# The forget gate's block between the two query blocks of a two-layer kernel, and a new order of VectorE's and ScalarE's work after it

## The chip, the cores and the metric

One core of one Trainium2 chip runs the whole kernel. The metric is the time on the device in microseconds (us); lower is better.

## The reference, cut to what matters

Two transformer blocks run one after the other on 512 tokens of width 1024, in float32. The change lies at the start of the second block, where its input `x` (the first block's normed output) is normed again and multiplied by the large matrix `w_in`:

```python
h = rms_norm_2(x, norm_mix_g[l])
proj = h @ w_in[l]
cb, cc, cin, q, k, v, f_logit, g_logit = jnp.split(proj, split_idx, axis=-1)   # widths 512 x6, 8, 2048
u = causal_dwconv(cc * cin, conv_mix_w[l])
y_conv = (cb * u) @ w_out_conv[l]
log_f = jax.nn.log_sigmoid((f_logit + b_f[l]).astype(jnp.float32))
o = forgetting_attention(q, k, v, log_f)        # adds F[query] - F[key], F = cumsum(log_f)
gates = jax.nn.sigmoid(g_logit + b_gate[l])
```

## The kernel before, in words

**Tiling.** Tokens lie along the free dimension (`xT`, 8 chunks of 128 features by 512 tokens). The weights pass in *slabs*, numbered in the order in which TensorE uses them. A whole A slab holds 1024 rows by 256 columns, a half one 512 rows by 256 columns. Every float32 product is made of three matmuls on rounded parts: a slab comes by DMA, ScalarE rounds it into `w_hi` (L975), VectorE subtracts to get `w_lo` (L1521), and TensorE multiplies hi x hi, hi x lo and lo x hi. `w_hi` and `w_lo` hold four half slabs each, as a ring: `MIX_FREES[e]` names the slabs whose place in the ring slab `e` gives back, so they are split only once slab `e` is finished (`slab_done`), and TensorE waits for `w_lo_ready` ahead of each slab.

**Order around the change.** Each engine's program is written out by hand, in one strict order, and the engines meet by semaphores. On TensorE: two key slabs (S_K2, S_K2+1), two sums of squares, query slab S_Q2, `turn_row` (four matmuls of one column, into bank 7), query slab S_Q2+1, the forget gate's slab S_F2 (1024 rows by 128 columns, 24 matmuls of 512 columns; bank 6), and then the *pairs*. A pair `i` is 512 output columns computed in seven half slabs p0 to p6 of 24 matmuls of 256 columns each (a Strassen-like scheme that saves one product in eight), with the order p0,i p3,i-1 p2,i p5,i-1 p1,i p6,i-1 p4,i. Pairs 0 to 2 are `cc`, `cin` and `cb`, 3 to 6 the gates. Within pair 5 four whole slabs `out,0` to `out,3` (24 matmuls of 512 columns each) multiply by `w_out_conv`. The values' slab S_V2 and the attention follow.

**What a pair needs.** The products p1, p3, p4, p5 work on sums of blocks of the gained input `xg2` (four subtractions at L1968 to L1974, rounded by ScalarE at L1235 into `s2_hi`, the rest by VectorE at L1978 into `s2_lo`). The weights of p1, p3 and p6 of a pair are made by accumulating DMAs on GpSimd's queue (L905): each adds to the slab before it in the chain p0, p1, p3, p6, and waits for that slab's `w_lo`; p5 adds to p4 in the same way. VectorE recombines: after p2 it writes one part from PSUM (L2013, `z_n0`), which p0 of the next pair waits for; after p3, `z_rest` (L2018) and `z_m0` (L2020), which p1 of the next pair waits for; after p5, `z_rest2` (L2024) and `z_m1` (L2027), for which ScalarE's copy of the next pair's p1 out of PSUM (L1218, `z_k1`) waits, and p4 waits for that copy; after p6, `z_n1` (L2032).

**What else VectorE does there.** It makes 1/rms of the new norm (L1943, L1945, the reciprocal L1544 `inverse(N_MIX2)`), scales keys (L1958) and queries (L1960) out of PSUM, forms the forget gate's log-sigmoid and its running sum (L1981 to L1992, with ScalarE's Abs, Exp and Ln at L1238 to L1242, after a table load), makes the final norm's reciprocal (`inverse(N_FINAL)`, L1544) and applies it to `xT` (`x_normal`, L1951), multiplies `cc` by `cin` (L2071), and adds the taps of the convolution (`taps`, L2048 and L2050), each at a place of the pairs' loop given by `X_NORMAL_AT` and `TAPS_AT`.

Of the kernel before, what the change touches and what calls it, by code (L numbers as in the profile page):

```python
# [20 lines left out]
P = 128  # L21
# [132 lines left out]
S_Q2 = _cols_a("w_in_2", 3 * WIDTH, WIDTH)  # L154
S_F2 = _add("w_in_2", "A", 0, DC, F_AT, P)
# [49 lines left out]
X_NORMAL_AT = {("p2", 0): (0, 1), ("p4", 0): (2, 3), ("p0", 1): (4, 5), ("p2", 1): (6, 7)}  # L205
TAPS_AT = {("p4", 2): 0, ("p0", 3): 1, ("p2", 3): 2}
# [61 lines left out]
def _z_landed(kind, i, stage):  # L268
# [23 lines left out]
for _s in range(N_SLABS):  # L292
    _inner = (_s in (S_V + 1, S_V2 + 1)
              or S_FFN + 1 < _s < S_DOWN
              or S_MIX <= _s < S_V2
# [71 lines left out]
def two_blocks(nc, t, out):  # L367
    with ExitStack() as ctx:
# [316 lines left out]
        def _(sp):  # L685
# [273 lines left out]
        def _(act):  # L959
# [240 lines left out]
            split_w(S_K2 + 3)  # L1200
# [41 lines left out]
            A(fsum[:, 1], fsum[:, 1], ACT.Ln, bias=1.0).then_inc(f_ln, 1)  # L1242
            for e in range(S_MIX, S_V2):
# [5 lines left out]
                if (kind, i) == ("p4", FIRST_GATE):  # L1249
# [238 lines left out]
        def _(dve):  # L1488
# [464 lines left out]
            for s in range(S_K2, S_F2):  # L1953
                finished(s)
                c0 = (s - S_K2) % 2 * 2
                for j in range(2):
                    if s < S_Q2:
                        ins = V.tensor_tensor(k2[:, c0 + j], bank(s, j), both, ALU.mult)  # L1958
                    else:
                        ins = V.scalar_tensor_tensor(q2[:, c0 + j], bank(s, j), SCALE, both, ALU.mult, ALU.mult)  # L1960
                free(ins)
                if s >= S_Q2:
                    for f in MIX_FREES[s]:
                        split_w(f)
                if s == S_Q2 - 1:
                    dve.wait_ge(xg_ready, 2 * DC)
                    h00, h01, h10, h11 = xg2_block(0, 0), xg2_block(0, 1), xg2_block(1, 0), xg2_block(1, 1)
                    V.tensor_tensor(h11, h01, h11, ALU.subtract).then_inc(sums_made, 1)  # L1968
                    dve.wait_ge(sums_made, 5)
                    V.tensor_tensor(h01, h01, h00, ALU.subtract).then_inc(sums_made, 1)  # L1970
                    dve.wait_ge(sums_made, 6)
                    V.tensor_tensor(h00, h00, h11, ALU.subtract).then_inc(sums_made, 1)
                    dve.wait_ge(sums_made, 7)
                    V.tensor_tensor(h10, h10, h00, ALU.subtract).then_inc(sums_made, 1)  # L1974
                if s == S_Q2:
# [1099 lines left out]
```

## Time and profile before

| | |
|---|---|
| three timed runs | 1266.15, 1271.99, 1279.71 us, median 1271.99 |
| the profiled execution | 1270.42 us, of which 1268.7 us are the span of the profile |
| TensorE busy in the span | 97% |
| mean granted clock of TensorE | 0.994 of full speed |

The profile is of one execution. Its times are counted from the span's start. TensorE's columns are *PE* (matmuls) and *PEld* (weight loads); DVE is VectorE, ACT ScalarE, POOL GpSimd, SP SyncE. A matmul's end is modelled, so the distance between the starts of two matmuls is what counts.

### The profile page before, as it was taken

The numbers are of one execution on the slowest core, as the hardware profiler recorded it, in microseconds if no ns is written. First come the engines' busy times: TensorE is split into PE (matmuls) and PEld (weight loads), VectorE is DVE, ScalarE is ACT, GpSimd is POOL, SyncE is SP. The second block draws the span as 40 slices with busy tenths as digits, with TensorE's granted clock in tenths as the row PEclk, the third lists the DMA queues.
The fourth block names the chain that finished last, engine by engine and source line by source line (L and its number), as shares of the span: only waits on it lengthen the run. The fifth ranks groups of instructions, "written<-read, shape, count | busy, mean of one in ns | idle before, by whom it ended". The sixth has DMA issues, their size and how long they took to land.

```text
span 1268.7 us, 19160 instructions
## 1 busy us (share of the span) xinstructions
PE 1235.8 (97%) x7805; PEld 1084.5 (85%) x7805; DVE 993.8 (78%) x1199; ACT 668.4 (53%) x832; POOL 185.9 (15%) x168
## 2 busy tenths in 40 slices
PE   6999999999999999999999999999999999999997
PEld 5778777889999999997899999657888999998886
DVE  6788764878878688987889867566678898979896
ACT  5462674374445346557433535363344665656555
POOL 4003010002222111200212212000000222201020
PEclk9999999999999999999899999999999999999999
DMA  5422201259999589653499957301324798958765
GB/s 170 141 67 100 67 1 34 97 138 182 198 183 187 114 239 280 107 114 117 86 197 189 194 100 193 122 3 34 116 84 149 132 211 186 178 141 180 211 111 138
DMA packets 144442, 174.14 MB, mean 137 GB/s; under 512 B 5354, under 2 KB 118234, under 8 KB 144226
## 3 DMA queue, kind: packets, MB, share of 16 engines
q0 software_dynamic: 58288, 71.33, 34.8%
q1 hardware_dynamic: 86050, 101.58, 23.9%
q8 instruction: 62, 1.02, 0.3%
q14 instruction: 26, 0.21, 0.1%
q10 hardware_dynamic: 16, 0.00, 0.0%
HBM read 170.78 MB, written 2.11 MB: 136 GB/s over the span
## 4 chain that ended last, share of the span: by engine, by line
PE 86%; DVE 7%; ACT 4%; issue 2%; DMA 1%; DVEq 0%; SPq 0%; ACTq 0%
PE psum L2456 11%; PE psum L2458 11%; PE psum L2457 11%; PE psum L2719 10%; PE psum L2721 10%; PE psum L2720 10%; PE psum L2791 3%; PE psum L2793 3%; PE psum L2792 3%; PE psum L2993 2%; PE psum L2994 2%; PE psum L2995 2%; PE psum L2902 1%; PE psum L2594 1%; PE psum L2579 1%
## 5 line engine op out<-in xcount | busy, mean ns | idle before, releaser
L975 ACT ACTIVATE w_hi<-raw 128x1024 fp32r<-128x1024 f32 (+2 forms) x121 | 157.2, 1301 | 214.8 <-PE psum L2458 148.9
L1521 DVE TENSOR_TENSOR w_lo<-raw,w_hi 128x1024 fp32r<-128x1024 f32 (+2 forms) x121 | 185.7, 1536 | 58.5 <-ACT w_hi L975 58.5
L2456 PE MATMUL psum<-act_hi,w_hi 128*128 128x512 f32 x520 | 209.1, 402 | 5.9 <-DVE act_lo L1530 1.7
L2458 PE MATMUL psum<-act_hi,w_lo 128*128 128x512 f32 x520 | 205.5, 395 | 0.0
L2457 PE MATMUL psum<-act_lo,w_hi 128*128 128x512 f32 x520 | 204.5, 393 | 0.0
L2719 PE MATMUL psum<-s_hi,w_hi 128*128 128x256 f32 x704 | 195.5, 278 | 1.3 <-issue 1.3
L2721 PE MATMUL psum<-s_hi,w_lo 128*128 128x256 f32 x704 | 195.2, 277 | 0.0
L2720 PE MATMUL psum<-s_lo,w_hi 128*128 128x256 f32 x704 | 195.1, 277 | 0.0
L2719 PE MATMUL psum<-act_hi,w_hi 128*128 128x256 f32 x528 | 147.6, 280 | 3.0 <-DVE conv_p L2013 2.7
L2720 PE MATMUL psum<-act_lo,w_hi 128*128 128x256 f32 x528 | 147.1, 279 | 0.0
L2721 PE MATMUL psum<-act_hi,w_lo 128*128 128x256 f32 x528 | 147.1, 279 | 0.0
L2719 PEld LDWEIGHTS psum<-s_hi,w_hi 128*128 128x128 f32 x704 | 132.1, 188 | 1.7 <-issue 1.4
L2721 PEld LDWEIGHTS psum<-s_hi,w_lo 128*128 128x128 f32 x704 | 132.2, 188 | 0.0
L2720 PEld LDWEIGHTS psum<-s_lo,w_hi 128*128 128x128 f32 x704 | 132.0, 187 | 0.2
L2456 PEld LDWEIGHTS psum<-act_hi,w_hi 128*128 128x128 f32 x520 | 98.4, 189 | 32.5 <-issue 6.7
L2457 PEld LDWEIGHTS psum<-act_lo,w_hi 128*128 128x128 f32 x520 | 98.4, 189 | 22.8 <-issue 1.7
L2458 PEld LDWEIGHTS psum<-act_hi,w_lo 128*128 128x128 f32 x520 | 98.3, 189 | 21.1
L2719 PEld LDWEIGHTS psum<-act_hi,w_hi 128*128 128x128 f32 x528 | 99.9, 189 | 3.9 <-issue 3.6
L2720 PEld LDWEIGHTS psum<-act_lo,w_hi 128*128 128x128 f32 x528 | 99.7, 189 | 0.3
L2721 PEld LDWEIGHTS psum<-act_hi,w_lo 128*128 128x128 f32 x528 | 99.9, 189 | 0.0
L1521 DVE TENSOR_TENSOR w_lo<-xz,w_hi 128x1024 fp32r<-128x1024 f32 x60 | 73.3, 1221 | 26.2 <-ACT w_hi L975 26.1
L975 ACT ACTIVATE w_hi<-xz 128x1024 fp32r<-128x1024 f32 x60 | 63.4, 1057 | 42.5 <-PE psum L2721 23.1
(413 smaller groups left out, 2690.3 us busy)
## 6 DMA issues: line engine op xcount, KB each, us to landing
raw<-in_w_in SPq DMA_DIRECT2D x16, 1024.0 KB, 5.2
xz<-in_w_ffn_in POOLq DMA_DIRECT2D x24, 512.0 KB, 6.4
raw<-in_w_ffn_in SPq DMA_DIRECT2D x22, 512.0 KB, 5.1
xz<-in_w_up POOLq DMA_DIRECT2D x21, 512.0 KB, 6.0
raw<-in_w_up SPq DMA_DIRECT2D x18, 512.0 KB, 5.0
raw<-in_w_in SPq DMA_DIRECT2D x15, 512.0 KB, 5.2
v<-in_w_in POOLq DMA_DIRECT2D x15, 512.0 KB, 6.5
x_buf<-in_w_ffn_out POOLq DMA_DIRECT2D x6, 1024.0 KB, 9.9
```

What stands on the lines that cost most here:

```text
L975: A(w_at(w_hi, s, h, n - h), home(s, n)[:, h:n], ACT.Copy).then_inc(w_hi_ready, 1)
L1521: V.tensor_tensor(w_at(w_lo, s, h, n - h), home(s, n)[:, h:n], w_at(w_hi, s, h, n - h).bitcast(F32), ALU.subtract).then_inc(w_lo_ready, 1)
L2456: mm(dst, stationary[0], moving[0], start=first, stop=False)
L2457: mm(dst, stationary[0], moving[1], start=False, stop=False)
L2458: return mm(dst, stationary[1], moving[0], start=False, stop=last)
L2719: mm(dst, wh, hi, start=kind not in ("p2", "p4") and k == 0 and m == 0, stop=False, skip_group_check=True)
L2720: mm(dst, wh, lo, start=False, stop=False, skip_group_check=True)
L2721: ins = mm(dst, wl, hi, start=False, stop=True, skip_group_check=True)
L2791: mm(dst, wh, hi, start=fresh, stop=False, skip_group_check=True)
L2792: mm(dst, wh, lo, start=False, stop=False, skip_group_check=True)
L2793: return mm(dst, wl, hi, start=False, stop=True, skip_group_check=True)
L2993: mm(dst, hi, wh, start=fresh, stop=False, skip_group_check=True)
```

## The change

The forget gate's slab S_F2 moves from behind the second query slab to between the two; its weights land in a place of their own (`v2[:, 2:4]`) instead of `raw`. The second query slab becomes two half slabs (S_Q2B and the next), computed by `quarter_slab`, in banks 0 and 1, as before. `turn_row` moves behind S_F2. VectorE and ScalarE follow a new order: VectorE splits S_F2 and the first half of the second query slab before the rms; then both keys, two splits, the first queries, the forget gate's start, the sums of `xg2`, and the rest of the gate between the `s2_lo` operations, which now come in the order 0, 3, 2, 1. ScalarE does its part of the forget gate ahead of rounding the sums. In the pairs, `inverse(N_FINAL)` moves from behind p1,0 to behind p4,0, `x_normal` from p2,0 p4,0 p0,1 p2,1 (two chunks each) to p0,1 (two), p4,1 and p0,2 (three each), the last taps from p2,3 to p4,3, the convolution's last product from p6,2 to p0,4, and its splitting from p4,3 to p5,3 (ScalarE) and p1,4 (VectorE). TensorE's order and its waits in the pairs are the same. At the end, S_V2's first products take their banks in the order 0, 2, 3, 1, and only bank 1 waits for `z_rest2`.

```diff
 S_K2 = _cols_a("w_in_2", 4 * WIDTH, WIDTH)
-S_Q2 = _cols_a("w_in_2", 3 * WIDTH, WIDTH)
-S_F2 = _add("w_in_2", "A", 0, DC, F_AT, P)
+S_Q2 = _cols_a("w_in_2", 3 * WIDTH, COLS_A)
+S_F2 = _add("w_in_2", "A", 0, DC, F_AT, P, ("z", ("f", 0), 2))
+S_Q2B = _add("w_in_2", "A", 0, WC, 3 * WIDTH + COLS_A, COLS_A)
+_add("w_in_2", "A", WC, WC, 3 * WIDTH + COLS_A, COLS_A)
...
-X_NORMAL_AT = {("p2", 0): (0, 1), ("p4", 0): (2, 3), ("p0", 1): (4, 5), ("p2", 1): (6, 7)}
-TAPS_AT = {("p4", 2): 0, ("p0", 3): 1, ("p2", 3): 2}
+X_NORMAL_AT = {("p0", 1): (0, 1), ("p4", 1): (2, 3, 4), ("p0", 2): (5, 6, 7)}
+TAPS_AT = {("p4", 2): 0, ("p0", 3): 1, ("p4", 3): 2}
+LO_ORDER = (0, 3, 2, 1)
...
+    if g == GROUP[S_F2]:
+        return OUT_BANKS[0]
+    if g == GROUP[S_Q2B]:
+        return bank_of(GROUP[S_K2 + 1])
     return 2 if g == GROUP[S_Q2] else 4 * (g % 2)
...
-            for s in range(S_K2, S_MIX):
+            for s in (S_K2, S_K2 + 1, S_Q2, S_Q2B):
                 load_slab(s)
             sp.wait_ge(slab_done, S_K2)
+            for s in (S_F2, S_Q2B + 1):
+                load_slab(s)
...
-                        sp.wait_ge(w_lo_ready, S_Q2 + 2 + i)
+                        sp.wait_ge(w_lo_ready, S_Q2B + 2 if i else S_Q2B + 1 if kind == "p4" else S_K2 + 2)
...
-            split_w(S_K2 + 3)
+            split_w(S_F2)
+            split_w(S_Q2B)
...
-            for s in range(S_Q2, S_MIX):
-                for f in MIX_FREES[s]:
-                    split_w(f)
-                if s == S_Q2:
-                    for k, (kh, th) in enumerate(SUM_PLACE):
-                        act.wait_ge(sums_made, 4 + k + 1)
-                        A(s2_hi[k].rearrange("p (k n) -> p k n", k=WC), xg2_block(kh, th), ACT.Copy).then_inc(sums_hi_ready, 1)
+            for f in MIX_FREES[S_Q2]:
+                split_w(f)
...
+            for k, (kh, th) in enumerate(SUM_PLACE):
+                act.wait_ge(sums_made, 4 + k + 1)
+                A(s2_hi[k].rearrange("p (k n) -> p k n", k=WC), xg2_block(kh, th), ACT.Copy).then_inc(sums_hi_ready, 1)
+            for s in range(S_F2, S_MIX):
+                for f in MIX_FREES[s]:
+                    split_w(f)
...
-                if (kind, i) == ("p4", FIRST_GATE):
+                if (kind, i) == ("p5", FIRST_GATE):
...
             for s in (S_K2, S_K2 + 1):
                 finished(s)
                 split_w(s + 2)
+            split_w(S_Q2B)
...
-            for s in range(S_K2, S_F2):
...
-                if s >= S_Q2:
-                    for f in MIX_FREES[s]:
-                        split_w(f)
-                if s == S_Q2 - 1:
...
-                if s == S_Q2:
...
+            keys(S_K2)
+            keys(S_K2 + 1)
+            finished(S_Q2)
+            for f in MIX_FREES[S_Q2]:
+                split_w(f)
+            queries(S_Q2, 0)
             finished(S_F2)
             free(V.tensor_tensor(fsum[:, 0], psum[0:HEADS, OUT_BANKS[0]], rstd[0:HEADS, RSTD_AT[N_MIX2]], ALU.mult))
             settle()
             V.tensor_scalar(fsum[:, 0], fsum[:, 0], f_bias[:, 0:1], None, ALU.add).then_inc(f_pre, 1)
...
+            dve.wait_ge(xg_ready, 2 * DC)
+            h00, h01, h10, h11 = xg2_block(0, 0), xg2_block(0, 1), xg2_block(1, 0), xg2_block(1, 1)
+            V.tensor_tensor(h11, h01, h11, ALU.subtract).then_inc(sums_made, 1)
...
+            sum_lo(0)
...
+            sum_lo(1)
+            for s in (S_F2, S_Q2B):
+                finished(s)
+                for f in MIX_FREES[s]:
+                    split_w(f)
+            finished(S_Q2B + 1)
+            queries(S_Q2B, 2)
+            for f in MIX_FREES[S_Q2B + 1]:
+                split_w(f)
+            sum_lo(2)
+            sum_lo(3)
...
+                    if i == 0:
+                        dve.wait_ge(sums_lo_ready, 8)
...
-                if (kind, i) == ("p1", 0):
+                if (kind, i) == ("p4", 0):
                     inverse(N_FINAL)
...
-                if (kind, i) == ("p6", 2):
+                if (kind, i) == ("p0", FIRST_GATE + 1):
...
-                if (kind, i) == ("p4", FIRST_GATE):
+                if (kind, i) == ("p1", FIRST_GATE + 1):
...
-                    for tb in range(TB):
+                    for tb in first if k == 0 else range(TB):
+                        if k == 0:
+                            ahead(tb)
...
-            for s in range(S_K2, S_F2):
...
+            for s in (S_K2, S_K2 + 1, S_Q2):
                 wait_banks(GROUP[s])
                 slab_a(s, **(dict(q=C_MIX2, order=MIX2_ORDER) if s == S_K2 else {}))
                 if s == S_K2 + 1:
...
-                if s == S_Q2:
-                    pe.wait_ge(rstd_ready, TURN[N_MIX2] + 1)
-                    turn_row(rstd[:, RSTD_AT[N_MIX2]], bank_of(GROUP[S_K2]) + 3)
             pe.wait_ge(root_done, TURN[N_FINAL] + 1)
-            slab_a(S_F2, bank=OUT_BANKS[0])
+            slab_a(S_F2)
+            pe.wait_ge(rstd_ready, TURN[N_MIX2] + 1)
+            turn_row(rstd[:, RSTD_AT[N_MIX2]], bank_of(GROUP[S_K2]) + 3)
+            wait_banks(GROUP[S_Q2B])
+            for n in range(2):
+                quarter_slab(f"q{n}", S_Q2B + n, (bank_of(GROUP[S_Q2B]), bank_of(GROUP[S_Q2B]) + 1))
 
             def mix_product(kind, i):
...
-                    pe.wait_ge(z_rest, n - 1) if i else wait_freed(GROUP[S_Q2 + 1])
+                    pe.wait_ge(z_rest, n - 1) if i else wait_freed(GROUP[S_Q2B])
...
-                    pe.wait_ge(sums_lo_ready, 4 + SUM_OF[kind] + 1)
+                    pe.wait_ge(sums_lo_ready, 4 + LO_ORDER.index(SUM_OF[kind]) + 1)
...
-            pe.wait_ge(z_rest2, PAIRS)
-            slab_v(S_V2, 0)
+            pe.wait_ge(z_rest, PAIRS)
+            slab_v(S_V2, 0, first=(0, 2, 3, 1), ahead=lambda tb: pe.wait_ge(z_rest2 if tb == 1 else z_rest, PAIRS))
```

## Rows read from the trace of the kernel before

**Rows 1.** The page's first part: busy time by engine.

```profile
PE 1235.8 (97%) x7805; PEld 1084.5 (85%) x7805; DVE 993.8 (78%) x1199; ACT 668.4 (53%) x832; POOL 185.9 (15%) x168
```

**Rows 2.** TensorE's waits, 595 to 800: total us, times, longest us.

```profile
PE psum L2719 <- DVE conv_p L2013: 2.7, 1, 2.7
PE psum L2456 <- DVE k L1958: 1.5, 1, 1.5
PE psum L2719 <- issue: 1.3, 1, 1.3
PE psum L2519 <- DVE rstd L1544: 0.9, 1, 0.9
PE psum L2456 <- DVE tmp L2024: 0.6, 1, 0.6
```

**Rows 3.** Stages (start:end length, busy per engine, PEclk, DMA share, GB/s).

```profile
600.35:603.90 3.55, 1.22 (x10) 0.97 (x9) 3.52 (x6) 2.00 (x2) 0.00 (x0) 0.82 0.41 131
603.90:609.18 5.28, 5.28 (x12) 4.18 (x13) 5.18 (x5) 3.56 (x4) 0.00 (x0) 0.50 0.00 0
636.84:641.25 4.41, 4.41 (x25) 4.41 (x26) 4.41 (x6) 0.00 (x0) 0.00 (x0) 0.62 1.18 238
641.25:692.12 50.87, 50.87 (x434) 50.87 (x433) 44.03 (x55) 21.66 (x23) 11.69 (x10) 1.00 0.90 179
696.38:722.18 25.80, 25.75 (x217) 25.58 (x217) 24.45 (x28) 17.04 (x21) 7.48 (x6) 1.00 1.04 196
722.18:787.68 65.50, 65.50 (x482) 61.51 (x480) 41.30 (x47) 26.81 (x30) 11.40 (x11) 1.00 0.66 130
```

**Rows 4.** TensorE in order of time: start, us, instruction, idle before it.

```profile
589.59 0.39 PE L2457 MATMUL psum<-act_lo,w_hi 128*128 128x512 f32 x1
600.12 0.40 PE L2458 MATMUL psum<-act_hi,w_lo 128*128 128x512 f32 x1
...
601.38 1.05 PE L2519 MATMUL psum<-ident,rstd 128*128 128x1 f32 x8 [0.87 <-DVE rstd L1544]
...
1026.24 0.35 PE L2719 MATMUL psum<-act_hi,w_hi 128*128 128x256 f32 x1 [0.28 <-ACT scratch L1340]
```

**Rows 5.** VectorE in order of time, from the rms to the pairs.

```profile
595.77 0.68 DVE L1943 TENSOR_SCALAR rstd<-psum 128x512 f32<-128x512 f32 x1
...
601.36 2.48 DVE L1958 TENSOR_TENSOR k<-psum,rstd 128x512 f32<-128x512 f32 x4
...
609.87 1.22 DVE L1521 TENSOR_TENSOR w_lo<-raw,w_hi 128x1024 fp32r<-128x1024 f32 x1
...
612.14 4.62 DVE L1978 TENSOR_TENSOR s_lo<-xg,s_hi 128x1024 fp32r<-128x1024 f32 x4
...
627.84 0.68 DVE L1989 SCALAR_TENSOR_TENSOR fsum<-fsum 8x512 f32<-8x512 f32 x1 [2.10 <-ACT fsum L1242]
...
632.62 3.34 DVE L1544 RECIPROCAL rstd<-rstd 128x512 f32<-128x512 f32 x1
...
636.00 0.69 DVE L2013 TENSOR_TENSOR conv_p<-psum,rstd 128x512 f32<-128x512 f32 x1
...
637.74 1.41 DVE L1951 SCALAR_TENSOR_TENSOR xT<-xT,par,rstd 128x512 f32<-128x512 f32 x2
...
691.54 2.72 DVE L2050 SCALAR_TENSOR_TENSOR conv_u<-conv_p,par,conv_u 128x510 f32<-128x510 f32 x4
```

**Rows 6.** ScalarE in order of time.

```profile
591.56 1.90 ACT L975 ACTIVATE w_hi<-raw 128x2048 fp32r<-128x2048 f32 x1
600.61 1.06 ACT L975 ACTIVATE w_hi<-raw 128x1024 fp32r<-128x1024 f32 x1 [2.10 <-PE psum L2458]
...
695.69 0.60 ACT L1218 ACTIVATE tmp<-psum 128x512 f32<-128x512 f32 x1 [5.07 <-DVE gc L2027]
```

**Rows 7.** Accumulating DMAs issued at 612.51 and at 631.93 and after: KB, median us to landing.

```profile
v<-in_w_in POOLq DMA_DIRECT2D x1, 512.0 KB, 6.9
...
v<-in_w_in POOLq DMA_DIRECT2D x2, 512.0 KB, 9.7
```

More of the change, by code:

```diff
@@ L273, in _z_landed @@
         return (("rz_in", 1), ("second_in", 0), ("rz_in", 0))[i]
+    if kind == "f":
+        return "second_in", 1
     if i == 1 and stage == 0:
@@ L294 @@
               or S_FFN + 1 < _s < S_DOWN
-              or S_MIX <= _s < S_V2
+              or S_Q2B < _s < S_V2
               or S_DOWN <= _s < S_DOWN + N_PARTS and _s not in (S_DOWN, S_DOWN + 9)
@@ L599, in home @@
                     return (mix_chain(i) if stage == 2 else xz[z_chain(i, stage)])[:, 0:n]
+                if kind == "f":
+                    return mix_chain(1)[:, 0:n]
                 if kind == "out":
@@ L1951, in x_normal, with keys @@
                 mark(V.scalar_tensor_tensor(xT[:, c], xT[:, c], col("norm_final", c), R(N_FINAL), ALU.mult, ALU.mult))
-            for s in range(S_K2, S_F2):
-                finished(s)
-                c0 = (s - S_K2) % 2 * 2
+            def keys(s):
                 for j in range(2):
[L1957 to L1960, printed above, removed]
+                    ins = V.tensor_tensor(k2[:, (s - S_K2) * 2 + j], bank(s, j), both, ALU.mult)
@@ L1961, in _ @@
                 free(ins)
-                if s >= S_Q2:
-                    for f in MIX_FREES[s]:
-                        split_w(f)
-                if s == S_Q2 - 1:
[L1966 to L1974, printed above, removed]
@@ L1975, in _, with queries @@
-                if s == S_Q2:
-                    for k, (kh, th) in enumerate(SUM_PLACE):
-                        dve.wait_ge(sums_hi_ready, 4 + k + 1)
-                        V.tensor_tensor(s2_lo[k].rearrange("p (k n) -> p k n", k=WC), xg2_block(kh, th),
-                                        s2_hi[k].rearrange("p (k n) -> p k n", k=WC).bitcast(F32), ALU.subtract).then_inc(sums_lo_ready, 1)
+            def queries(s, c0):
+                for j in range(2):
+                    ins = V.scalar_tensor_tensor(q2[:, c0 + j], bank(s, j), SCALE, both, ALU.mult, ALU.mult)
+                free(ins)
@@ new lines, in sum_lo @@
+            def sum_lo(n):
+                k = LO_ORDER[n]
+                kh, th = SUM_PLACE[k]
+                dve.wait_ge(sums_hi_ready, 4 + k + 1)
+                V.tensor_tensor(s2_lo[k].rearrange("p (k n) -> p k n", k=WC), xg2_block(kh, th),
+                                s2_hi[k].rearrange("p (k n) -> p k n", k=WC).bitcast(F32), ALU.subtract).then_inc(sums_lo_ready, 1)
+            keys(S_K2)
[3 more added lines that the diff above has]
+                split_w(f)
@@ L1983, in _ @@
             V.tensor_scalar(fsum[:, 0], fsum[:, 0], f_bias[:, 0:1], None, ALU.add).then_inc(f_pre, 1)
-            for f in MIX_FREES[S_F2]:
-                split_w(f)
+            dve.wait_ge(xg_ready, 2 * DC)
+            h00, h01, h10, h11 = xg2_block(0, 0), xg2_block(0, 1), xg2_block(1, 0), xg2_block(1, 1)
+            V.tensor_tensor(h11, h01, h11, ALU.subtract).then_inc(sums_made, 1)
+            dve.wait_ge(sums_made, 5)
+            V.tensor_tensor(h01, h01, h00, ALU.subtract).then_inc(sums_made, 1)
+            dve.wait_ge(sums_made, 6)
+            V.tensor_tensor(h00, h00, h11, ALU.subtract).then_inc(sums_made, 1)
+            dve.wait_ge(sums_made, 7)
+            V.tensor_tensor(h10, h10, h00, ALU.subtract).then_inc(sums_made, 1)
             dve.wait_ge(row_turned, 2)
             V.tensor_copy(small[:, 52:52 + TB], psum[:, bank_of(GROUP[S_K2]) + 3, 0:TB]).then_inc(row_read, 1)
+            sum_lo(0)
             dve.wait_ge(f_ln, 1)
@@ L2493, in slab_b, with slab_v @@
                 ins.then_inc(slab_done, 1)
-            def slab_v(s, part, before=lambda k: None):
+            def slab_v(s, part, before=lambda k: None, first=range(TB), ahead=lambda tb: None):
                 wait_w(s)
```

## The prediction, made before the changed kernel ran

> **What bounds the kernel now.** I read the busy times first: TensorE is busy for 97% of the span, VectorE for 78% [rows 1]. So the work of TensorE, which the change leaves the same in number and size of matmuls, sets the time, and only what stands between its matmuls can be won. Next come its waits in the stretch that the change touches: 0.9, 1.5, 2.7, 1.3 and 0.6 us, 7.0 in all [rows 2]. Last, the table of stages, where a stall is seen to cost more than its length, in two ways [rows 3]. First, the clock: from 603.90 to 609.18 the granted clock is 0.50, the level of 1.2 GHz, after a stretch in which TensorE did little but `turn_row`; 636.84 to 641.25 has 0.62 after the wait for L2013. Second, the cadence of the 256-column stream. From 722.18 to 787.68 lie 16 half slabs and four `out` slabs. An `out` slab has 24 matmuls of 512 columns, whose starts are (600.12 - 589.59) / 46 = 0.229 apart, 5.50 in all [rows 4]; so a half slab takes (65.50 - 22.0) / 16 = 2.72. But from 641.25 to 692.12, at full clock and without a wait, 18 half slabs take 50.87, 2.826 each, and 696.38 to 722.18 is no faster [rows 3]. After a stall the stream stays 4% slower, until a slab of 512 columns comes.
>
> **TensorE from the end of S_Q2 to the pairs.** S_Q2 ends at 600.35 in the order of starts, and p0,1 starts at 636.84: 36.49. The work in between is 72 matmuls of 512 columns (16.5), `turn_row` (1.05, [rows 4]) and four half slabs (10.9), 28.4 in all. The other 8.1 are the waits of 0.9 and 1.5, the half clock (12 matmuls at twice 0.229, about 2.6) and the 2.7 ahead of p0,1. After the change S_F2 follows S_Q2 at once. Its `w_lo` is early: ScalarE now makes two halves of 1.06 from 591.56 on instead of one of 1.90, and VectorE two of 1.14 instead of one of 2.29, which overlap better, so L1943 starts at 594.98, 0.8 earlier than at 595.77 [rows 5, 6]. The reciprocal's end and the keys move by the same 0.8; the keys run 600.57 to 603.05. S_F2 keeps TensorE until 605.85, `turn_row` until 606.9; both the keys' banks and the half slab's `w_lo` are ready by then, and I expect no wait and no half clock. The two half slabs of queries end at 617.9, p0,0 p1,0 p2,0 p4,0 at 628.8.
>
> **Does VectorE keep up until p0,1?** From 603.05: two splits (2.27, the distance of 609.87 and 612.14 in [rows 5], where two stand), two queries 1.2 (each costs about an L2013), the gate's two small operations 1.3, the four subtractions 5.0 (128x1024 like a split, with a semaphore between them), a copy 0.1, one `s2_lo` 1.15: 614.0. ScalarE's table load and Abs, Exp, Ln take 3.25 from 607.8 and are done at 611.0; its rounding of the sums follows and is done by 614.9. The scan's group takes 2.47: 616.4. One `s2_lo`, then p1,0's `w_lo` at 617.6 to 618.7 (TensorE wants it at 620.6), p2,0's, queries, p4,0's at 622.2 (wanted at 626.1), two `s2_lo`, p0,1's `w_lo`: 625.6. Now comes the narrow place. p3,0's weights are an accumulating DMA behind p1,0's `w_lo`; issued at 618.8 with 6.9 to 9.7 to landing [rows 7]. I take the lower, nearly unloaded one, 7.1 with the semaphores: 625.9. ScalarE 1.06, VectorE's split 1.14, and only then, in VectorE's order, L2013 of p2,0 (0.69): `z_n0` at 628.9, so p0,1 starts at 629.1, 0.3 after TensorE is free, against 636.84 before: **-7.8**. The 2.7 of the old wait came from the reciprocal of 3.34 in front of L2013 [rows 2, 5]; it now stands behind p4,0.
>
> **From p0,1 to `out,0`.** Before: 722.18 - 636.84 = 85.34 for 29 half slabs. At the fast cadence they take 78.9, at the slow one 81.95. A gap of 0.28 at 1026.24 [rows 4] is followed by 90 us at the slow cadence in the same trace, so my 0.3 ahead of p0,1 is enough for the slow one. It still saves 3.4: the half clock of 636.84 to 641.25 (4.41 - 2.83 = 1.6), the wait ahead of p4,3 (1.3 in [rows 2] and 0.1 of refill) and 0.4 of small ones behind it. That wait ends at 696.38 and is put down to issue; but what ended at 696.29 was ScalarE's copy L1218, which had waited 5.07 for L2027 [rows 6], and L2027 stood behind the taps of 2.72 at p2,3 [rows 5]. The taps move behind p4,3.
> The Trainium skill ("TensorE: Matmul & The Clock Gate", step-by-step, on LDWEIGHTS) says that TensorE's queue pulls weight loads ahead of matmuls that are in flight. By that rule alone the stream would regain 2.72 a slab after a stall, and the stretch would take 78.9; the trace has 2.826 over 18 slabs without a wait, so the sum goes by the row.
>
> **Does VectorE keep up in the pairs?** From 628.2 to `z_m0` of p3,2, which p1,3 waits for, it has 17 splits (19.4), the recombining of nine products (19 operations of 0.69 with a little overlap, 12.7) and 1.4 of a tenth, the reciprocal 3.35, `x_normal` 8 x 0.66 = 5.3, L2071 2.3, and taps 1.6 and 2.65: 48.7 without a pause, so 676.9, and about 679.3 with the pauses that I find for ScalarE and DMA. TensorE comes to p1,3 at 629.1 + 18 x 2.826 = 680.0. It holds, by 0.7. Every other place is looser: p1,1 and p4,1 by 1.8, p1,2 and p4,2 by 1.5, p1,4 by 1.3, `out,0` (the last `z_lo` at 708.7) by 2.3. So `out,0` starts at 711.0 against 722.18. From there VectorE and ScalarE have idle time and TensorE none, and 65.50 stays.
>
> **The end of the pairs.** 787.68 to 788.45 is the wait of 0.6 for L2024 and the refill [rows 2]. With banks 0, 2 and 3 first, TensorE has 9 matmuls of 0.229, 2.1, before it needs it: **-0.8**. The extra split and DMA (one slab became two) cost 0.2 of VectorE each way and lie in the sum above.
>
> **Sum.** -7.8 - 3.4 - 0.8 = -12.0. On the profiled execution 1270.4 - 12.0 = 1258.4; that execution is 1.6 under the median, so on the median 1272.0 - 12.0 = **1260 us**, 0.94% faster.
>
> **Rivals.**
> *The fast cadence is kept.* If p3,0's DMA lands half a us earlier, p0,1 doesn't wait. TensorE would reach p1,3 at 677.8 and then meet VectorE at 679.3, so `out,0` is at 708.8 to 709.7, not 707.7. If the stream regained 2.72 after the stall of 0.3, p1,3 would be held at the same 679.3 and the time be the same. The sum is -13.2 to -14.2: about 1258. The bound without any idle time or slow cadence is 107.3 of work in the 121.83 from 600.35 to `out,0`, with the end -15.3: 1256.7. For it: 40 of the pairs' slabs elsewhere run at 2.72. Against it: the margin is nil in my walk. The second way to it is the page's rule on weight loads, named above.
> *A late DMA gives part back.* With 9.7 to landing, the value that [rows 7] show where the DMA engines are crowded, p0,1 starts 2.6 later than above, the clock falls as it did after 2.7 (1.6), and VectorE is 2.6 later at p1,3, where TensorE by then is also later. -12.0 + 2.6 + 1.6 = -7.8: 1264. For it: the loads of p0,0, p2,0, p4,0 and p0,1 come earlier, and p2,1's and p4,1's too. Against it: these have landed by 610, and the DMA share from 603.90 to 609.18 was 0 [rows 3].
> *Slower than before.* VectorE becomes the bound from p0,1 to `out,0`. Its 48.7 lie in 51.7 of TensorE's time; if its operations beside the denser stream took 8% more, p1,3 would wait, and each us on top is lost. To be slower than before they must take 12 + 0.7 more, 25% longer. Before, at 95% busy (24.45 of 25.80 from 696.38 on, [rows 3]), they took no longer than elsewhere. By 15% it would be 1267, by 25% 1272 and over.
>
> **How the numbers follow.** Forecast 0.50, fast cadence 0.22, late DMA 0.24, slower or no gain 0.04. The range holds from the bound without idle time, less 1 for the noise of a median, to the late DMA with as much again of stalls of its kind: 1255 to 1268. About 1% (12.7 us) is what a measurement of this kernel tells from no change. Faster by over that: the fast cadence and a quarter of the forecast, 0.35. Within it: 0.62. Slower: 0.03.
>
> **What would show each step.** In the profile after: no row of a granted clock of 0.5 between S_Q2 and the pairs; TensorE without a wait from S_Q2 to p0,1, which starts near 629; half slabs of 2.83 or 2.72 after it; no wait before p4,3; `out,0` near 711; no wait for L2024. I am wrong if `turn_row` between two slabs lets the clock fall, if p0,1 or p1,3 waits for more than a us, or if the times after `out,0` don't simply move.

## The result, and the profile after

| | before | after |
|---|---|---|
| median, us | 1270.44 (20 runs, 1264.95 to 1281.61) | 1261.68 (20 runs, 1258.74 to 1274.49) |
| profiled execution, us | 1270.42 | 1258.74 |

The ratio is 0.9942, with a 95% interval of 0.9915 to 0.9968: the change makes the kernel about 0.6% faster. A second comparison, with the same kernel run as c1_after_again, gave 0.9889 (0.9857 to 0.9922). What lets two comparisons differ this much is taken up in the section on the cadence below.

The profile of after, busy time by engine (beside [rows 1]):

```profile
PE 1228.9 (98%) x7805; PEld 1078.8 (86%) x7805; DVE 993.6 (79%) x1200; ACT 667.6 (53%) x833; POOL 186.3 (15%) x168
```

TensorE's waits of after from 595 to 800 (total us, times, longest us), beside [rows 2]:

```profile
PE psum L2757 <- issue: 1.4, 1, 1.4
PE psum L2492 <- issue: 0.5, 1, 0.5
```

Five waits of 7.0 us have become two of 1.9. The stages of after, in the columns of [rows 3]; they run from `turn_row`, just behind S_F2, to p0,0, to p0,1, to p1,4, to `out,0`, and to the values' slab:

```profile
605.39:617.28 11.89, 11.89 (x57) 9.91 (x56) 11.55 (x15) 8.87 (x10) 1.09 (x1) 1.00 0.52 127
617.28:628.59 11.31, 11.31 (x98) 11.31 (x96) 10.56 (x11) 5.33 (x6) 5.58 (x5) 1.00 0.79 106
628.59:700.80 72.21, 70.83 (x602) 70.64 (x601) 65.81 (x79) 30.27 (x33) 16.84 (x14) 1.00 1.01 205
700.80:712.19 11.39, 11.38 (x96) 11.39 (x97) 11.29 (x15) 8.59 (x12) 2.59 (x2) 1.00 0.88 160
712.19:774.98 62.79, 62.79 (x459) 58.83 (x457) 40.68 (x48) 27.26 (x32) 10.27 (x8) 1.00 0.71 136
```

The granted clock is 1.00 in every row: the two stretches at the level of 1.2 GHz are gone. TensorE in order of time, at `turn_row` and at the two waits that are left (beside [rows 4]):

```profile
605.39 0.95 PE L2557 MATMUL psum<-ident,rstd 128*128 128x1 f32 x8
...
700.80 0.36 PE L2757 MATMUL psum<-s_hi,w_hi 128*128 128x256 f32 x1 [1.39 <-issue]
...
778.34 0.47 PE L2492 MATMUL psum<-w_hi,act_hi 128*128 128x512 f32 x1 [0.48 <-issue]
```

**Where the 11.7 us between the two profiled executions went.** I cut the stretch at five starts on TensorE: S_Q2's first product, p0,0, p0,1, `out,0`, and the values' first product.

| us | S_Q2 to p0,0 | to p0,1 | to `out,0` | to the values | sum |
|---|---|---|---|---|---|
| before | 33.86 | 13.77 | 85.34 | 66.27 | 199.24 |
| after | 28.53 | 11.31 | 83.60 | 66.15 | 189.59 |
| difference | -5.33 | -2.46 | -1.74 | -0.12 | -9.65 |

The prediction had -7.8 for the first two columns together, -3.4 for the third and -0.8 for the last. The other -2.0 lie outside the stretch, in code that is the same: -0.5 ahead of it and -1.6 behind it. The -1.6 is no gain of the change: c1, the same kernel in another execution, takes 480.2 behind the stretch, as before does, and after takes 478.6.

### The profile page after: what moved, and what is told of

Read it like the earlier page. It is cut to its first block, busy times and chain, and to the rows that moved or that the text cites. A ratio compares the mean times of both kernels' runs of the same rounds, so it can differ in the third digit from the quotient of the medians.

```text
span 1257.0 us, 19170 instructions
## 1 busy us (share of the span) xinstructions
PE 1228.9 (98%) x7805; PEld 1078.8 (86%) x7805; DVE 993.6 (79%) x1200; ACT 667.6 (53%) x833; POOL 186.3 (15%) x168
## 4 chain that ended last, share of the span: by engine, by line
PE 95%; ACT 2%; DVE 2%; issue 1%; DMA 1%; SPq 0%; ACTq 0%
PE psum L2492 12%; PE psum L2494 12%; PE psum L2493 12%; PE psum L2758 11%; PE psum L2757 11%; PE psum L2759 11%; PE psum L3035 3%; PE psum L3034 3%; PE psum L3033 3%; PE psum L2829 3%; PE psum L2830 3%; PE psum L2831 3%; PE psum L2942 1%; PE psum L2632 1%; PE psum L2617 1%; PE psum L2644 1%
```

## Experiments

**Theories.** A: the front and the pairs are two separate gains, each to be had alone. B: they hang together, since a faster TensorE in the front meets VectorE's old order in the pairs, and a new order in the pairs can't keep a gain while the front is late. The wait of 1.39 that is left at p1,4 gave a third question: who holds it. The runs of after that lie near 1270 gave a fourth: what else sets the time.

### The front alone, and its parts taken back one at a time

e1_front_only is after with the three edits of the pairs taken back; each of the next three takes back one.

```diff
 e2_reciprocal_early
-X_NORMAL_AT = {("p0", 1): (0, 1), ("p4", 1): (2, 3, 4), ("p0", 2): (5, 6, 7)}
+X_NORMAL_AT = {("p2", 0): (0, 1), ("p4", 0): (2, 3), ("p0", 1): (4, 5), ("p2", 1): (6, 7)}
-                if (kind, i) == ("p4", 0):
+                if (kind, i) == ("p1", 0):
                     inverse(N_FINAL)
 e3_taps_early: taps 2, the last product and both splits at their old places
-TAPS_AT = {("p4", 2): 0, ("p0", 3): 1, ("p4", 3): 2}
+TAPS_AT = {("p4", 2): 0, ("p0", 3): 1, ("p2", 3): 2}
 e4_tail_back
-            pe.wait_ge(z_rest, PAIRS)
-            slab_v(S_V2, 0, first=(0, 2, 3, 1), ahead=...)
+            pe.wait_ge(z_rest2, PAIRS)
+            slab_v(S_V2, 0)
```

> The changed kernel with only the front kept: the forget gate's block between the query blocks and the order of VectorE and ScalarE up to p0,0; in the pairs the reciprocal of the final norm, x_normal, taps and the convolution's splitting are back in their old places, and so is the order of the banks at the end. My theory: most of the gain comes from the front, but the reciprocal (3.35 us) stands again between p3,0's split and L2013 of p2,0. p3,0's split is held by its DMA until about 27 us after S_Q2's end, so p0,1 starts 1.8 us later than in the changed kernel: 30.5 us after the end of S_Q2, against 28.7 there and 36.5 before. The clock stays up. The wait of 1.4 ahead of p4,3 is back, the one of 1.4 ahead of p1,4 is gone. Device time 9 us under the kernel before. Rival: the pairs' order carries the gain; then p0,1 is at 34 us or more after S_Q2 with the clock down, and the time is within 4 us of the kernel before.

> The changed kernel with one thing undone: the final norm's reciprocal and x_normal are back behind p1,0 and p2,0 p4,0 p0,1 p2,1. My theory: a wait of about 1.8 us ahead of p0,1 (30.5 us after S_Q2's end instead of 28.7), no fall of the clock, later waits in the pairs as in the changed kernel or shorter. Rival: with VectorE's backlog only shifted, p0,1 waits as long as before (2.7) and the clock falls behind it, which would cost 1.6 more; then 'behind p4,0' is what makes the front pay.

> The changed kernel with the last taps back at p2,3 and the convolution's product and splits back at p6,2 and p4,3. My theory: the wait of 1.4 us ahead of p4,3 comes back and the one of 1.4 ahead of p1,4 goes, so the stretch from p0,1 to out,0 is the same within 0.5 us (83.6): the step that I priced at 1.4 only moved the stall. Rival: both waits are there, because VectorE is the bound either way, and the stretch is 1.4 longer.

> The changed kernel with the old order of banks at the first values product and its wait for z_rest2. In the changed kernel a wait of 0.5 stayed there though the wait for z_rest2 was gone. My theory: the split of the values' slab (2.3 us on VectorE, ending at the same moment) holds TensorE, so the old order costs only 0.1 to 0.2 us more: out,0 to the first values product 66.3 instead of 66.15. Rival: the wait that stayed is something else (issue), and the old order adds the whole 0.6 to it.

Measured: e1 1270.77 (10 runs), ratio 0.9969 (0.993 to 1.0007), not told apart from before, where 9 us had been expected. The others had one execution each: 1273.3, 1267.39, 1272.99. TensorE's waits from 595 to 800 in e1:

```profile
PE psum L2757 <- DVE conv_p L2049: 2.3, 1, 2.3
PE psum L2757 <- issue: 1.3, 1, 1.3
PE psum L2492 <- DVE tmp L2060: 0.7, 1, 0.7
```

The same in e2:

```profile
PE psum L2757 <- DVE conv_p L2049: 2.3, 1, 2.3
PE psum L2757 <- issue: 0.8, 1, 0.8
```

With the reciprocal at its old place, p0,1 waits 2.3 for p2,0's `z_n0`, in both, and in both the clock falls behind it, where 1.8 and no fall had been expected. The half slab p0,1 in e1, then in e2, in the columns of [rows 3] (24 matmuls that take 2.83 without this):

```profile
636.88:641.27 4.39, 4.39 (x25) 4.39 (x26) 4.39 (x6) 0.00 (x0) 0.00 (x0) 0.62 1.13 258
640.82:645.12 4.30, 4.30 (x24) 4.30 (x25) 4.30 (x6) 0.00 (x0) 0.00 (x0) 0.64 1.12 256
```

So e2's rival came true, with 2.3 in place of its 2.7: the reciprocal's new place is needed for the front to pay in full. VectorE in e1 shows the one operation that stands in between:

```profile
631.52 1.23 DVE L1536 TENSOR_TENSOR w_lo<-v,w_hi 128x1024 fp32r<-128x1024 f32 x1 [0.70 <-ACT w_hi L988]
632.66 3.35 DVE L1559 RECIPROCAL rstd<-rstd 128x512 f32<-128x512 f32 x1
```

Stretch by stretch (table below), two of the parts, taken back, cost at their own places: e2 ahead of p0,1, and e3 ahead of p4,3, where the taps are early; it waits 2.4 there, the clock falls behind it, and nothing waits at p1,4. That is 86.13 to `out,0` where e3's theory had 83.6 and its rival 1.4 more. In e4 the wait for L2060 is back at the tail, and 66.38 stand where after has 66.15 and c1, the same kernel, 65.75: one profile each doesn't show the price of the tail's order. e4's 86.53 to `out,0` are not of its edit, which comes later; they are taken up below.

The last column counts, of the 49 half slabs from p0,0 on, those that took over 2.8 us from their first start to the next product's. Most of them run at the slow cadence; up to three in a row of the table are there for a wait or a half clock.

| us | to p0,0 | to p0,1 | to `out,0` | to the values | sum | half slabs over 2.8 |
|---|---|---|---|---|---|---|
| before | 33.86 | 13.77 | 85.34 | 66.27 | 199.24 | 31 |
| c2 (before again) | 32.89 | 13.84 | 85.35 | 67.38 | 199.46 | 49 |
| after | 28.53 | 11.31 | 83.60 | 66.15 | 189.59 | 34 |
| c1 (after again) | 28.55 | 11.31 | 83.52 | 65.75 | 189.13 | 34 |
| e1 front only | 28.55 | 13.77 | 85.30 | 66.36 | 193.98 | 34 |
| e2 reciprocal early | 28.56 | 13.76 | 84.60 | 65.75 | 192.67 | 34 |
| e3 taps early | 28.52 | 11.31 | 86.13 | 67.19 | 193.15 | 49 |
| e4 tail back | 28.54 | 11.31 | 86.53 | 66.38 | 192.76 | 32 |
| e5 pairs only | 33.97 | 10.88 | 86.93 | 67.31 | 199.09 | 42 |
| e6 taps first | 28.53 | 11.31 | 82.59 | 65.68 | 188.11 | 34 |
| e7 and tail | 28.55 | 11.31 | 84.08 | 65.51 | 189.45 | 33 |
| e8 and product | 28.55 | 11.31 | 84.12 | 67.25 | 191.23 | 49 |
| e9 and `turn_row` | 27.62 | 11.31 | 82.87 | 67.25 | 189.05 | 49 |

### The unchanged kernel once more, and the pairs alone

> The changed kernel once more, nothing edited. What is asked: how much of the span is the change's and how much is the matmul stream's cadence. My theory: from the first product of S_Q2 to the first values product it takes 189.6 to 192.8 us (199.2 before) with no wait up to p0,1; outside that stretch its streams of 256-column matmuls run at 2.72 or at 2.83 us a half slab, not always as in its first profile, and that alone moves the span by up to 15 us. Rival: the stretches outside repeat within 1 us, and the differences between profiles come from the edits.

c1: 1261.43 (7 runs, 1260.47 to 1263.48). Its stretch agrees with that of after to 0.5 us, wait at p1,4 (1.3) included. Ahead of it both long streams run at the fast cadence, as in after; behind it c1 takes 1.6 more, with half slabs slow from 1018 on that are fast up to 1060 in after. That the streams ahead of it vary too, as the theory had it, is seen only in e1, e2, e4 and e8.

e5_pairs_only is before with nothing but the new order of the pairs:

```diff
...
-                if (kind, i) == ("p1", 0):
+                if (kind, i) == ("p4", 0):
                     inverse(N_FINAL)
...
-                if (kind, i) == ("p6", 2):
+                if (kind, i) == ("p0", FIRST_GATE + 1):
...
```

> The kernel before with only the pairs' new order (reciprocal, x_normal, taps, the convolution's product and splits); the front and the end are as before. My theory: the waits and the half clock around the second query slab (about 5 us) stay, S_Q2's first product to p0,0 is 33.9 us; the wait of 2.7 ahead of p0,1 goes, since L2013 of p2,0 no longer stands behind the reciprocal, so S_Q2's first product to p0,1 is 44.8; behind it a wait ahead of p4,3 of 0 and one ahead of p1,4 of 0 to 2.4. Device time 3 to 6 us under the kernel before. Rival: without the front VectorE is later, and p0,1 waits all the same.

e5: 1271.84 (10 runs), ratio 1.0 (0.9966 to 1.0035), where a gain of 3 to 6 us had been expected. The wait ahead of p0,1 is gone: p0,0 and what comes ahead of p0,1 take 33.97 + 10.88 = 44.85 against 47.63 before. But the gain is given back behind it. TensorE in e5, the two places:

```profile
647.15 0.36 PE L2719 MATMUL psum<-s_hi,w_hi 128*128 128x256 f32 x1 [0.88 <-issue]
...
709.25 0.35 PE L2719 MATMUL psum<-s_hi,w_hi 128*128 128x256 f32 x1 [1.94 <-issue]
```

The stage behind the second one in e5:

```profile
709.25:713.50 4.25, 4.25 (x23) 4.25 (x24) 4.21 (x6) 2.53 (x5) 0.32 (x1) 0.60 0.81 162
```

The wait of 1.94 is followed by a granted clock of 0.60, which is worth 1.7 more (4.25 by 0.4), so it costs 3.6. VectorE in e5 ahead of it:

```profile
700.43 1.23 DVE L1521 TENSOR_TENSOR w_lo<-raw,w_hi 128x1024 fp32r<-128x1024 f32 x1 [2.54 <-ACT w_hi L975]
701.57 2.72 DVE L2050 SCALAR_TENSOR_TENSOR conv_u<-conv_p,par,conv_u 128x510 f32<-128x510 f32 x4
```

**A or B?** In the sums B seems to hold: the front alone is worth 199.24 - 193.98 = 5.3, the pairs alone 0.15, both 9.65. Place by place it is less clear.

- *To p0,1 the gains are separate, as A says.* The first two columns change by -5.3 and 0.0 in e1, by 0.1 and -2.9 in e5, and by -5.3 and -2.5 in after.
- *To `out,0` they aren't:* 0.0 in e1, 1.6 more in e5, 1.7 less in after. But the wait at p1,4, which makes e5's loss, is the one that after has too, with the same cause (next section). From p0,1 to p1,4 it takes 74.0 in e5, 72.2 in after, and 73.9 in e4, whose code there is that of after. So e5 loses no more than the new order of the pairs can lose with the new front, and that the old front makes VectorE late in the pairs is not shown.
- *The last column* is 1.0 more in e5, as it is in c2, the kernel before, at the slow cadence.
- *The times* (ratios of 0.9969 and 1.0 alone, 0.9942 or 0.9889 together) don't decide it, given their intervals.

What does show one wait handing over to the next is e1 beside e3. They differ in the reciprocal's place and in the tail. With it moved, the wait of 2.3 and the half clock at p0,1 are gone, and the wait at p4,3 grows from 1.3 to 2.4 and gets a half clock: TensorE comes earlier and VectorE's taps still stand in the way.

### Who holds p1,4

VectorE in after, ahead of p1,4:

```profile
688.04 1.22 DVE L1536 TENSOR_TENSOR w_lo<-raw,w_hi 128x1024 fp32r<-128x1024 f32 x1
...
691.98 1.23 DVE L1536 TENSOR_TENSOR w_lo<-raw,w_hi 128x1024 fp32r<-128x1024 f32 x1 [2.71 <-ACT w_hi L988]
693.12 2.73 DVE L2086 SCALAR_TENSOR_TENSOR conv_u<-conv_p,par,conv_u 128x510 f32<-128x510 f32 x4
695.76 1.22 DVE L1536 TENSOR_TENSOR w_lo<-v,w_hi 128x1024 fp32r<-128x1024 f32 x1
696.89 2.36 DVE L2113 TENSOR_TENSOR conv_u<-conv_u,gc 128x1024 f32<-128x1024 f32 x2
699.28 0.69 DVE L2054 TENSOR_TENSOR tmp<-psum,tmp 128x512 f32<-128x512 f32 x1
700.01 0.69 DVE L2056 TENSOR_TENSOR gc<-psum,tmp 128x512 f32<-128x512 f32 x1
```

ScalarE in after, what VectorE waits for:

```profile
690.82 1.06 ACT L988 ACTIVATE w_hi<-raw 128x1024 fp32r<-128x1024 f32 x1 [4.37 <-DMA raw<-in_w_in]
```

L2056 writes `z_m0`, which p1,4 waits for; it ends at 700.7 and p1,4 starts at 700.80. The profile puts the wait down to issue, but its chain is: an accumulating DMA (8.0 from issue to landing), ScalarE's rounding, VectorE's split, and then 7.6 us of VectorE's own work, two thirds of it (taps and product) of no use to p1,4. VectorE is busy for most of the stretch, yet idle 2.71 just before it becomes the one that is late. Without this idle time it would be early by 1.3, the margin that the prediction gave it. In e4, whose code is that of after up to the tail, the same DMA took 9.4, ScalarE waited 5.83 for it, p1,4 waited 2.4, and the clock fell:

```profile
711.78:717.00 5.22, 5.22 (x31) 5.22 (x32) 5.15 (x7) 2.72 (x6) 1.28 (x1) 0.67 0.79 167
```

So this place costs 1.4 in one execution and 4.1 (2.4 and 5.22 by 0.33) in another of the same code. The DMA issued from 680 to 690 in after, and from 688 to 702 in e4 (KB, us to landing):

```profile
raw<-in_w_in POOLq DMA_DIRECT2D x1, 512.0 KB, 8.0
```

```profile
raw<-in_w_in POOLq DMA_DIRECT2D x1, 512.0 KB, 9.4
```

e6 lets VectorE do the taps in its idle time, ahead of the split; e7 adds the same thought for the tail, where S_V2's `w_lo` (not `z_rest2`) holds TensorE in after; e8 adds the product.

```diff
 e6_taps_first
+                if (kind, i) == ("p4", 3):
+                    taps(TAPS_AT[(kind, i)])
                 for f in MIX_FREES[e]:
                     split_w(f)
...
 e7_taps_first_and_tail: S_V2 is split behind z_rest of the last p3, and ScalarE's sigmoids of pair 5 behind its rounding
+                    if i == MIXES - 1:
+                        for f in MIX_FREES[mix_at("p3", i)]:
+                            split_w(f)
...
 e8_product_first
+                if (kind, i) == ("p0", FIRST_GATE + 1):
+                    settle()
+                    for c in (0, 2):
+                        V.tensor_tensor(conv_u[:, c:c + 2], conv_u[:, c:c + 2], gc[:, 4 + c:6 + c], ALU.mult).then_inc(src_ready, 2)
...
                 for f in MIX_FREES[e] if (kind, i) != ("p3", MIXES - 1) else ():
...
```

> The changed kernel with one thing moved: the last taps (2.7 us) stand ahead of the split of p5,3's weights at p4,3, not behind it. In the changed kernel VectorE idles 2.7 us there for these weights (a DMA that lands late) and the taps come after. My theory: the wait ahead of p1,4 (1.4 to 2.4 us, once with a fall of the clock) goes, and p0,1 to out,0 takes 82.0 at the slow cadence, 1.6 to 4.5 us less than in the profiles of the changed order. Rival: the split then comes late enough for p5,3 itself to wait, and nothing is won.

> The last one, and the values' slab split earlier: on VectorE right behind z_rest of p3,6, on ScalarE ahead of the sigmoids of pair 5. My theory: that split, not z_rest2, holds TensorE at the first values product; out,0 to the first values product falls from 66.15 to 65.5 and the wait there to nothing. Rival: the wait of 0.5 is of TensorE's own and stays.

> The kernel with the taps first and the values' slab split early, and now the convolution's last product (2.35 us on VectorE) ahead of the split of p1,4's weights at p0,4 too, where VectorE idled 1.7 to 1.9 us for that slab's accumulating DMA. My theory: these two idle times of VectorE behind late DMAs, with work put behind them, are what makes z_m0 of p3,3 late; the wait ahead of p1,4 (1.4 us, 0.4 with only the taps first in one profile) is gone, and from S_Q2's first product to the first values product it takes 187.5 us against 189.6. Device time 2 us under the changed kernel, 12 to 14 under the kernel before. Rival: VectorE has too much to do there in any order and the wait stays over 0.5.

Measured: e6 1265.44, ratio 0.9928 (0.9889 to 0.9968); e7 1261.39, 0.9923 (0.9884 to 0.9962), 10 runs each; e8 1260.65 (12 runs), 0.9933 (0.9908 to 0.9959). VectorE in e6:

```profile
688.53 2.73 DVE L2086 SCALAR_TENSOR_TENSOR conv_u<-conv_p,par,conv_u 128x510 f32<-128x510 f32 x4
691.32 1.23 DVE L1536 TENSOR_TENSOR w_lo<-raw,w_hi 128x1024 fp32r<-128x1024 f32 x1
...
694.27 1.23 DVE L1536 TENSOR_TENSOR w_lo<-v,w_hi 128x1024 fp32r<-128x1024 f32 x1 [1.72 <-ACT w_hi L988]
695.41 2.35 DVE L2115 TENSOR_TENSOR conv_u<-conv_u,gc 128x1024 f32<-128x1024 f32 x2
```

The taps do move into the idle time, and in this execution 0.4 is left of the wait and `out,0` is 1.0 earlier. In e7, with the same order here, the next split waited 1.90 with the product behind it, and the wait was 1.4 again. In e8, with the product moved too, nothing waits ahead of p1,4 any more, nor in e9 and e10, which keep this order. So VectorE's order held p1,4, as long as work of no use to it stood behind a late DMA. e8 pays elsewhere: 0.7 ahead of p6,3, for a `w_lo` that comes from another accumulating DMA, and 0.7 ahead of p4,4. Its stretch is 191.2, not the 187.5 expected.

At the tail no wait stands from e7 on, 65.51 against 66.15, as expected. But c1, e2 and e6, which still have after's tail, show 65.75, 65.75 and 65.68, and no wait in their lists: with that order it is there in some executions only, so e7's gain is 0.2 to 0.6. None of the three is told apart from after by its time.

### `turn_row` elsewhere

Half slabs ran at the slow cadence from p0,0 on in every profile of the new front. e9 tests whether `turn_row`, which stands just ahead of p0,0's stream, is the cause: it comes ahead of p0,5 there, and VectorE's copy of its result behind p4,4.

```diff
+                if (kind, i) == ("p0", MIXES - 2):
+                    pe.wait_ge(rstd_ready, TURN[N_MIX2] + 1)
+                    turn_row(rstd[:, RSTD_AT[N_MIX2]], bank_of(GROUP[S_K2]) + 3)
...
```

> The last one, and turn_row (four float32 matmuls of one column, and VectorE's copy of them) moved from ahead of the second query slab to ahead of p0,5. In the nine profiles with the new front in which it stands ahead of the queries, the half slabs from p0,0 on take 2.83 each, even where no wait came first; with the old front, where the clock fell behind it, 2.72. Theory: turn_row sets the slow cadence; then p0,0 to p4,4 take 2.72 each until VectorE becomes the bound, 1.5 to 3 us are saved, and the cadence is slow behind p0,5 only. Rival: the cadence is fixed by something else in the execution, and the half slabs still take 2.83; then there is no gain, and VectorE's wait for the row costs about 0.5.

> The kernel before once more, nothing edited, for a second profile of it. My theory: the waits of the stretch repeat (0.9, 1.5, 2.7, 1.3 and 0.6), from S_Q2's first product to the first values product it takes 199 us again within 1.5, and the cadence of the streams outside it may differ. Rival: this stretch itself varies by as much as the change moved it.

e9: 1264.21 (12 runs), ratio 0.9963 (0.9932 to 0.9994). It has no wait of TensorE between 595 and 800, the only one in the table, and the shortest way from S_Q2 to `out,0` (121.8; e6 122.4), but all its 49 half slabs are slow. `turn_row` isn't the cause. c2 (the kernel before, one execution of 1269.05) shows that the expectation started from a wrong premise too: there p0,0 was slow with the old front. Its stretch takes 199.46 as expected, with waits of 0.9, 1.5, 2.4 and 1.3; the one at the tail is missing.

### The cadence, and what it does to the time

Half slabs of 256-column matmuls run at one of two cadences at full clock and without waits: 0.1130 us a matmul or 0.1177 (2.72 or 2.83 a half slab). This is so in code far from the change. The stage 290 to 427, columns as in [rows 3], in the kernel before:

```profile
290.00:427.00 137.00, 137.00 (x1212) 137.00 (x1211) 111.79 (x131) 67.93 (x79) 37.24 (x29) 1.00 0.95 185
```

and in e8, whose code there is the same:

```profile
290.00:427.00 137.00, 137.00 (x1165) 137.00 (x1164) 108.57 (x125) 66.16 (x76) 35.96 (x28) 1.00 0.93 180
```

1212 against 1165 matmuls in the same 137 us, no idle time in either, clock 1.00 in both. Ahead of the change lie two such streams, of about 51 and 38 half slabs. The start of S_Q2's first product sorts by their cadence alone:

| both fast | first slow | both slow |
|---|---|---|
| 588.3 to 590.4 (before, after, c1, c2, e3, e5, e6, e7, e9, e10) | 594.56 (e1) | 598.50, 598.01, 599.28 (e2, e4, e8) |

89 half slabs by 0.105 are 9.3 us, about the distance between the two heaps of e8's timed runs, ten at 1258.98 to 1262.83 and two at 1269.97 and 1270.33 (the latter is the profiled one, both streams slow). Fifteen runs of after lie between 1258.7 and 1265.0 and five between 1269.6 and 1274.5. Of the kernel before, 3 of 20 runs lie over 1278 in the first comparison and 10 of 28 in c1's, while all seven of c1 lie under 1264: such shares alone move a ratio. Only one run of each is profiled, so that the cadence makes these heaps is likely, not shown. That e1, e2 and e4 were near 1272 says little of their edits; their stretches do.

What switches it? e10 puts two matmuls of 512 columns ahead of each p0 (e9 otherwise; their result is overwritten by p0's first matmul into that bank).

```diff
+                    for _ in range(2):
+                        mm(psum[:, UP_BANK[kind]], act_hi[:, 0, 0:P], act_hi[:, 0], start=True, stop=True)
```

> The kernel with turn_row late, and two matmuls of 512 columns more ahead of every p0 (their result is overwritten by p0; the output is the same). In most profiles the slow cadence of 2.83 a half slab ended at an out slab, which has 24 matmuls of 512 columns. Theory: any 512-column matmul in the stream can bring back the fast cadence; then the half slabs after one of these pairs take 2.72 in at least some of the pairs 0 to 5. Rival: two are not enough or width is not what ends it; then all of them stay at 2.83 up to out,0 and each of these additions costs 0.46 to 0.6 us.

e10: 1262.64 (one execution). Two stretches of 168 such matmuls, p0,1 to p4,1 and p0,2 to p4,2, each between two of the added pairs:

```profile
628.29:647.33 19.04, 19.04 (x170) 19.04 (x168) 17.10 (x18) 7.85 (x9) 4.29 (x4) 1.00 1.09 237
647.79:667.58 19.79, 19.79 (x170) 19.79 (x169) 18.16 (x23) 8.52 (x9) 5.18 (x5) 1.00 0.99 188
```

0.1133 a matmul behind the first of these pairs, 0.1178 behind the next, fast again behind that of p0,4. In e9, which lacks them, all stay slow. So in this one execution the cadence changes either way at 512-column matmuls. From fast to slow it also goes after short gaps, and with none: in after it is fast through a gap of 0.37 at 1016, and turns slow at a start that came 0.15 behind the last instead of 0.11, with no wait. TensorE in after, there:

```profile
1059.72 0.28 PE L2759 MATMUL psum<-s_hi,w_lo 128*128 128x256 f32 x1
1059.83 0.31 PE L2757 MATMUL psum<-s_hi,w_hi 128*128 128x256 f32 x1
1059.98 0.28 PE L2758 MATMUL psum<-s_lo,w_hi 128*128 128x256 f32 x1
```

From slow to fast it went only at 512-column matmuls or after a change of the clock (e4, where half slabs of 2.83 up to the fall at p1,4 are followed by such of 2.72), in every profile. Why the new front always gave the slow cadence at p0,0 stays open, as does what a cadence is inside the engine.

## Why the prediction was right, and where not

The time was forecast as 1260, and 1261.68 was measured; the median of before moved too, from 1272.0 to 1270.4, so the gain was 8.8 (7.4 by the ratio, 4.1 to 10.8 by its interval) where 12.0 was forecast, a miss that the time alone would hide. That 1261.68 lies so near 1260 is in part luck: before's median came out 1.6 lower. Step by step:

- **The front: right, to the digit by luck.** -7.8 forecast, -7.79 measured in the stretch. The keys run from 600.12 (600.57 forecast), `turn_row` brings no fall of the clock, and p0,1 starts at 628.59 (629.1; this execution is 0.46 early). The wait of 0.3 didn't come: `z_n0` ended at 627.58, since the accumulating DMA took 6.1, less than the 6.9 that I had as its lower end [rows 7]. The margin was 1.0, not nil. Against that, p0,0 to p4,0 ran at the slow cadence, 11.31 where I had put 10.9. The two misses, 0.3 and 0.4, and 0.2 less for `turn_row` cancel. VectorE there:

```profile
625.76 1.23 DVE L1536 TENSOR_TENSOR w_lo<-v,w_hi 128x1024 fp32r<-128x1024 f32 x1 [0.75 <-ACT w_hi L988]
626.90 0.68 DVE L2049 TENSOR_TENSOR conv_p<-psum,rstd 128x512 f32<-128x512 f32 x1
```

- **The reciprocal behind p4,0: right**. e1 and e2 show the price of its old place: 2.5 ahead of p0,1 and the fall of the clock behind it, 1.5 more. VectorE kept up at p1,3, the place I had called the narrowest (0.7): no wait stands there.
- **p0,1 to `out,0`: right in kind, too large.** -3.4 forecast, -1.74 measured. The wait ahead of p4,3 is gone, the half clock too, and the cadence is the slow one as forecast. The step that failed is the sentence that every other place is looser, with 1.3 at p1,4: 29 half slabs at 2.83 and that wait of 1.39 are 83.3. I give only margins for it and no walk; one pause alone on the way, behind a DMA of 8.0, was 2.71. The rival *a late DMA gives part back* came in this smaller form, at p5,3's weights and not at p3,0's, where I had looked.
- **The slow cadence: right number by luck, wrong rule.** "After a stall the stream stays 4% slower, until a slab of 512 columns comes" fits before's page and not the rest: it is slow without any stall (after from p0,0 on, e8 from 289 on), survives a small gap as fast (after at 1016), and a slab of 512 columns may leave it slow (c2, e3, e5, e8, e9). My rival *the fast cadence is kept* hung on p3,0's DMA landing in time; it did, p0,1 didn't wait, and the stream was slow all the same, as it already was at p0,0.
- **The Trainium skill's rule** ("TensorE: Matmul & The Clock Gate", step-by-step) has weight loads run ahead of matmuls in flight; from that alone I had worked out that a stall would leave no slower pace behind. The traces show both cadences without idle time, 0.1130 and 0.1177, so that rule by itself doesn't give the stream's pace here.
- **The tail: mis-sized.** -0.8 forecast, -0.12 measured in after and -0.52 in c1. The bank order does take `z_rest2` off the path; in after 0.48 of wait is left for the values' `w_lo`, a wait that my sum doesn't have. TensorE's start at 778.34 follows the first of these two operations, not the second. VectorE in after:

```profile
775.96 2.28 DVE L1536 TENSOR_TENSOR w_lo<-raw,w_hi 128x2048 fp32r<-128x2048 f32 x1
778.16 0.68 DVE L2060 TENSOR_TENSOR tmp<-psum,tmp 128x512 f32<-128x512 f32 x1
```

e7, which splits earlier, has no wait there.

- **Not foreseen:** up to 10 us between executions from cadences in unchanged code. It is as large as the whole gain, and likely the reason why the range of 1255 to 1268 holds the median but not each run.

## What to carry to other kernels

Judge an edit of a few us by its own stretch, cut at instruction starts, in at least two profiles, and by the median of many runs; a single time of this kernel can be 10 us off for reasons that lie elsewhere. When a wait is removed, walk to the next one on the same engine: with the reciprocal moved and the taps not (e3), the wait of p0,1 went and the one of p4,3 grew from 1.3 to 2.4. An engine's order should put work that nobody waits for into its idle time ahead of a late transfer, not behind it; and where an operation waits for an accumulating DMA, carry its spread (5.8 to 11.2 us for 512 KB at several places of after's trace) rather than one value.

## What the runs showed of the hardware

- Two cadences of back-to-back 256-column matmuls at the same granted clock, 0.1130 and 0.1177 us, each held for 137 us and more. A change from slow to fast was seen only at 512-column matmuls or after a change of the clock (e4).
- Short waits can bring on the half clock: inside the pairs the clock fell after each wait of 2.7 (before), 2.4 (c2, e3, e4), 2.3 (e1, e2) and 1.94 (e5), and after one of 1.85 at 1021 in e3. It didn't fall after 1.4 in after and e7, nor after 1.3 in before, c1 and e1.
- With the DMA engines nearly always busy (shares of 0.96 from 680 to 690 in after, 1.01 from 688 to 702 in e4), the same accumulating DMA ahead of p5,3 took 8.0 in one execution and 9.4 in another.
